# One step of a hybrid GLA and HGRN2 decoder layer: the first norm's gain applied by feature out of PSUM, the low-rank unit in two passes, one diagonal step, levels in 32 columns

## What is computed

```python
h  = x + rms_norm(token_mix(rms_norm(x, norm_mix_pre)), norm_mix_post)
x' = h + rms_norm(swiglu(rms_norm(h, norm_ffn_pre)), norm_ffn_post)
```

```python
S_t = diag(a_t) S_{t-1} + k_t^T v_t ;  o_t = q_t S_t
scores[t, s] = sum_k q[t,k] k[s,k] exp(b[t,k] - b[s,k])   for s <= t, b = cumsum(log a)
```

## Time and profile before

| what | us |
|---|---|
| median of 3 runs | 1134.85 |
| lowest, highest | 1133.91, 1137.36 |
| the profiled execution | 1134.5 |
| its span | 1132.7 |
| PE (matmul) busy in it | 1084.6 |
| DVE busy | 680.1 |
| ACT busy | 479.9 |
| POOL busy | 51.2 |

### The profile page before, as it was taken

How to read it: one execution, slowest core, us unless ns; L and a number is a source line. 1 busy time by engine, 2 the same in 40 slices (tenths; PEclk the granted TensorE clock), 3 DMA queues, 4 the chain that set the end, 5 groups by cost and what they waited for, 6 DMA issues and landing times.

```text
span 1132.7 us, 24821 instructions
## 1 busy us (share of the span) xinstructions
PE 1084.6 (96%) x10860; PEld 1020.0 (90%) x10860; DVE 680.1 (60%) x977; ACT 479.9 (42%) x765; POOL 51.2 (5%) x78
## 2 busy tenths in 40 slices
PE   4999999999999999999999999789999999999998
PEld 4999999989999899999899977689999999988886
DVE  4255543565444655525655457699999999854544
ACT  4342244523335522445333443653444444533432
POOL 6000000100001000001000011000000000000000
PEclk8999999999999999999999999899999999999999
DMA  6532232522224522235222155024243333332212
GB/s 174 135 83 55 72 84 81 164 74 59 75 67 123 142 56 76 67 94 167 58 76 76 48 170 175 1 76 112 77 112 84 104 94 94 99 106 75 93 56 84
DMA packets 138619, 105.19 MB, mean 93 GB/s; under 512 B 3968, under 2 KB 123776, under 8 KB 138512
## 3 DMA queue, kind: packets, MB, share of 16 engines
q1 hardware_dynamic: 133648, 85.78, 26.9%
...
...
## 4 chain that ended last, share of the span: by engine, by line
PE 88%; DVE 6%; ACT 2%; DVEq 1%; ACTq 1%; issue 1%; DMA 1%; POOL 0%; POOLq 0%
PE ps L253 42%; PE ps L1663 19%; PE ps L1685 12%; PE ps L342 2%; PE ps L935 2%; PE ps L989 1%; PE ps L966 1%; PE ps L956 1%; PE ps L911 1%; PE ps L968 1%; PE ps L973 1%; PE ps L931 1%; ACT w_hi_t L239 1%; DVE w_lo_t L243 1%; PE ps L949 1%
## 5 line engine op out<-in xcount | busy, mean ns | idle before, releaser
L253 PE MATMUL ps<-x_hi,w_lo_t 128*128 128x288 f32 x1168 | 258.3, 303 | 4.1 <-DVE w_lo_t L243 4.1
L253 PE MATMUL ps<-x_lo,w_hi_t 128*128 128x288 f32 x1168 | 252.6, 298 | 0.0
L253 PE MATMUL ps<-x_hi,w_hi_t 128*128 128x288 f32 x1168 | 252.5, 298 | 0.0
L239 ACT ACTIVATE w_hi_t<-w_raw_t 128x1024 fp32r<-128x1024 f32 x73 | 77.2, 1058 | 353.3 <-PE ps L253 341.8
L243 DVE TENSOR_TENSOR w_lo_t<-w_raw_t,w_hi_t 128x1024 fp32r<-128x1024 f32 x75 | 91.7, 1222 | 188.2 <-ACT w_hi_t L239 188.2
L253 PEld LDWEIGHTS ps<-x_hi,w_lo_t 128*128 128x128 f32 x1168 | 189.5, 192 | 9.1 <-DVE w_lo_t L243 4.2
L253 PEld LDWEIGHTS ps<-x_hi,w_hi_t 128*128 128x128 f32 x1168 | 190.7, 191 | 0.0
L253 PEld LDWEIGHTS ps<-x_lo,w_hi_t 128*128 128x128 f32 x1168 | 190.5, 191 | 0.0
L1663 PE MATMUL ps<-x_hi,w_lo_t 128*128 128x288 f32 x264 | 78.7, 298 | 5.5 <-issue 4.1
L1663 PE MATMUL ps<-x_lo,w_hi_t 128*128 128x288 f32 x264 | 78.4, 297 | 0.0
L1663 PE MATMUL ps<-x_hi,w_hi_t 128*128 128x288 f32 x264 | 78.4, 297 | 0.0
...
## 6 DMA issues: line engine op xcount, KB each, us to landing
w_raw_t<-in_w_in_dram SPq DMA_DIRECT2D x73, 512.0 KB, 3.8
merged<-in_w_ffn_in_dram SPq DMA_DIRECT2D x22, 512.0 KB, 5.1
w_raw_t<-in_w_ffn_in_dram SPq DMA_DIRECT2D x22, 512.0 KB, 4.7
w_raw_t<-in_w_ffn_out_dram SPq DMA_DIRECT2D x22, 512.0 KB, 3.7
h_t<-in_x_prompt_dram SPq DMA_DIRECT2D x8, 512.0 KB, 6.0
...
h_t<-in_state_hgrn_dram POOLq DMA_DIRECT2D x8, 512.0 KB, 8.4
...
```

What stands on the lines that cost most here:

```text
L239: nc.scalar.activation(w_hi_t[:, u % NSPL, 0:nk, :], w_raw_t[:, u % NRAW, 0:nk, :], ACT.Copy).then_inc(w_hi, 1)
L253: m = nc.tensor.matmul(out[:, q, :], w[:, u % NSPL, k, :], x(k, q), start=first and i == 0, stop=last and i == len(todo) - 1)
```

## The change

1. *Gain.* The diagonals and their spreading over the partitions are gone. POOL multiplies a tile by 1/rms in place. PE transposes it, and DVE multiplies the transposed tile by the gain, which is then one number per partition and block k, from PSUM into SBUF (`gained_x`, in buffers that are unused so far). `x_hi` and `x_lo` are made from that. ACT's `x_hi` of tile c now comes after the squares of tile c + 3 (`LAG`), not c + 2.
2. *Low-rank unit.* POOL writes the low part of the 16 weights beside the high part in the same 128 columns (columns 16 to 31). So two passes, x_lo and x_hi, give high and low products in 32 rows; the decay matmul sums them with `wlr4` standing twice. It runs token tile by token tile (80 matmuls) into banks 6 and 7.
3. *Order of the start.* Unit 0's weights are loaded before the last token tile, unit 1's right behind it. POOL splits both units (high and low), between and after its scalings, and makes the masks last.
4. *Diagonal.* One step in place of three, its 54 matmuls packed in one PSUM slot by strips; DVE takes it in six copies.
5. *Levels 5 and 6.* Level 6 in matmuls of 32 columns, twice as many; in both, every second head lands in the other half of the partitions, so that all four strips are used. DVE takes them in twice as many copies of half the size.

```diff
-NOW = {2: ["decay"], 6: ["diag0", "diag1", "diag2"], 7: ["level0", "v0"], 8: ["level1", "v1"], 9: ["level2", "v2"],
+NOW = {2: ["decay"], 6: ["diag"], 7: ["level0", "v0"], 8: ["level1", "v1"], 9: ["level2", "v2"],
...
-    glr = A("glr", [GR, T])
-    wlr4 = A("wlr4", [GR, GH * P])
+    glr = A("glr", [2 * GR, T])
+    wlr4 = A("wlr4", [2 * GR, GH * P])
...
-    gains = O[:, :, :].rearrange("p a b -> p (a b)")[:, 0:D].rearrange("p (k n) -> p k n", k=KT)
-    gain_rows = ps[:, 6:8, :].rearrange("p a b -> p (a b)")
+    glr_out = ps[:, 6:8, :].rearrange("p a b -> p (a b)")
+    x_full = [t[:, :, :].rearrange("p a b -> p (a b)")[:, i * D:(i + 1) * D] for t, i in ((O, 0), (O, 1), (Gt, 0), (Gt, 1), (Q, 0))]
+
+    def gained_x(c):
+        return x_full[c][:, 0:KT * tok(c)].rearrange("p (k t) -> p k t", k=KT)
...
         for c in range(NT):
+            if c == NC:
+                load_unit(sp, 0, win_v[:, :, GLR:GLR + P])
             sp.dma_start(xt[c][0:tok(c), :], xp_v[c] if c < NC else xs_v).then_inc(x_in[c], 16)
-        load_unit(sp, 0, win_v[:, :, GLR:GLR + P])
+        load_unit(sp, 1, win_v[:, :, UNITS[0][0]:UNITS[0][0] + P])
...
+                     (onm[:, 0:2], gla_onorm), (onm[:, 2:3], hgrn_onorm), (blr4[:, :], gla_b_lr),
+                     (wlr4[0:GR, :], gla_w_lr2.rearrange("o r d -> (o r) d")), (wlr4[GR:2 * GR, :], gla_w_lr2.rearrange("o r d -> (o r) d"))):
...
+                if j == 0 and n == 0:
+                    continue
...
 
+        for c in range(NT):
+            if c == NC:
+                pool.wait_ge(w_raw[0], loaded(0))
+                nc.gpsimd.tensor_copy(w_hi_t[:, 0, :, :], w_raw_t[:, 0, :, :]).then_inc(w_hi, 1)
+                pool.wait_ge(w_hi, 1)
+                nc.gpsimd.tensor_tensor(w_hi_t[:, 0, :, GR:2 * GR], w_raw_t[:, 0, :, 0:GR], w_hi_t[:, 0, :, 0:GR].bitcast(F32),
+                                        ALU.subtract).then_inc(w_lo, 2)
+            pool.wait_ge(squared, c + 1)
+            nc.gpsimd.tensor_scalar(xt[c][0:tok(c), :], xt[c][0:tok(c), :], stat[0:tok(c), 1, c:c + 1], None, ALU.mult).then_inc(scaled, 1)
+        pool.wait_ge(w_raw[1], loaded(1))
+        nc.gpsimd.tensor_copy(w_hi_t[:, 1, :, :], w_raw_t[:, 1, :, :]).then_inc(w_hi, 1)
+        pool.wait_ge(w_hi, 2)
+        nc.gpsimd.tensor_tensor(w_lo_t[:, 1, :, :], w_raw_t[:, 1, :, :], w_hi_t[:, 1, :, :].bitcast(F32), ALU.subtract).then_inc(w_lo, 1)
         pool.wait_ge(consts, n)
-        pool.wait_ge(gain_in, 16)
-        for k in range(KT):
-            nc.gpsimd.tensor_scalar(gains[:, k, :], ident[:], gain[:, 0, k:k + 1], None, ALU.mult).then_inc(gain_diag, 1)
...
-        for u in range(2):
-            pool.wait_ge(w_raw[u % NRAW], loaded(u))
-            nc.gpsimd.tensor_copy(w_hi_t[:, u % NSPL, :, :], w_raw_t[:, u % NRAW, :, :]).then_inc(w_hi, 1)
...
-        for i in range(NT + 2):
+        for i in range(NT + LAG):
...
-            if i >= 2:
-                c = i - 2
-                act.wait_ge(turned, c + 1)
-                act.activation(x_hi[:, :, tokens(c)], turned_x(c), ACT.Copy).then_inc(x_hi_s, 1)
-        act.wait_ge(small, 16 * 5)
+            if i >= LAG:
+                c = i - LAG
+                act.wait_ge(gained, c + 1)
+                act.activation(x_hi[:, :, tokens(c)], gained_x(c), ACT.Copy).then_inc(x_hi_s, 1)
+        act.wait_ge(small, 16 * 6)
...
-        act.activation(halves(glr[:, :]), proj(0)[0:GR], ACT.Copy).then_inc(unit_free, 1)
+        act.activation(glr[:, :], glr_out[0:2 * GR, 0:T], ACT.Copy).then_inc(unit_free, 1)
...
+                    if j == 0:
+                        act.wait_ge(consts, CONSTS)
...
-        dve.drain().then_inc(w_lo, 1)
...
-        dve.wait_ge(gain_row, 1)
-        for i in range(NT + 2):
+        dve.wait_ge(gain_in, 16)
+
+        def gain_x(c):
+            dve.wait_ge(turned, c + 1)
+            dve.tensor_tensor(gained_x(c), turned_x(c), gain[:, 0, :].rearrange("p (k o) -> p k o", o=1).broadcast_to([P, KT, tok(c)]),
+                              ALU.mult).then_inc(gained, 1)
+
+        for i in range(NT + LAG - 1):
             if i < NT:
-                n = tok(i)
-                dve.wait_ge(squared, i + 1)
-                dve.scalar_tensor_tensor(xt[i][0:n, :], xt[i][0:n, :], stat[0:n, 1, i:i + 1], gain_rows[0:n, :],
-                                         ALU.mult, ALU.mult).then_inc(scaled, 1)
-            if i >= 2:
-                c = i - 2
+                gain_x(i)
+            if i >= LAG - 1:
+                c = i - LAG + 1
                 dve.wait_ge(x_hi_s, c + 1)
-                dve.tensor_tensor(x_lo[:, :, tokens(c)], turned_x(c), x_hi[:, :, tokens(c)].bitcast(F32), ALU.subtract).then_inc(x_lo_s, 1)
-            if i >= NT - 1 and i <= NT:
-                dve.wait_ge(w_hi, i - NT + 2)
-                split_lo(i - NT + 1)
-        dve.wait_ge(small, 16 * 5)
+                dve.tensor_tensor(x_lo[:, :, tokens(c)], gained_x(c), x_hi[:, :, tokens(c)].bitcast(F32), ALU.subtract).then_inc(x_lo_s, 1)
+        dve.wait_ge(small, 16 * 6)
         dve.wait_ge(w_hi, 3)
         split_lo(2)
...
-        dve.wait_ge(consts, CONSTS)
...
             if L >= 32:
                 for t in range(0, C, 2 * L):
-                    ins = dve.tensor_copy(Am[t:t + L, :, t + L:t + 2 * L],
-                                          s[t:t + L, 0:3 * NC * C // 2].rearrange("p (h r) -> p h r", r=C // 2)[:, :, t // 2:t // 2 + L])
+                    for up in (0, 1):
+                        ins = dve.tensor_copy(Am[t:t + L, up:3 * NC:2, t + L:t + 2 * L],
+                                              s[t + up * L:t + up * L + L, 0:3 * NC // 2 * L].rearrange("p (h r) -> p h r", r=L))
...
-        def diagonal(j, i):
-
-            s = step(j, f"diag{i}")
+        def diagonal(j):
+
+            s = step(j, "diag")
             one = ident[:, :].bitcast(I32).rearrange("p (o t) -> p o t", o=1)
-            if i < 2:
-                ins = dve.copy_predicated(Am[:, 6 * i:6 * i + 6, :], one.broadcast_to([P, 6, C]),
-                                          s[:, 0:6 * C].rearrange("p (h t) -> p h t", t=C))
-            else:
-                ins = dve.copy_predicated(As[:, :, :], one[0:TS, :, 0:TS].broadcast_to([TS, 3, TS]),
-                                          s[0:TS, 0:3 * TS].rearrange("p (h t) -> p h t", t=TS))
-            freed(ins, j, f"diag{i}")
+            for t in range(0, C, STRIP):
+                strip = slice(t, t + STRIP)
+                got = s[strip, 0:3 * NT * STRIP].rearrange("p (h t) -> p h t", t=STRIP)
+                if t < TS:
+                    dve.copy_predicated(As[strip, :, strip], one[strip, :, strip].broadcast_to([STRIP, 3, STRIP]), got[:, 3 * NC:3 * NT, :])
+                ins = dve.copy_predicated(Am[strip, :, strip], one[strip, :, strip].broadcast_to([STRIP, 3 * NC, STRIP]), got[:, 0:3 * NC, :])
+            freed(ins, j, "diag")
...
-                    for i in range(3):
-                        diagonal(j, i)
+                    if j == 0:
+                        dve.wait_ge(consts, CONSTS)
+                    diagonal(j)
                     dve.tensor_tensor(Q[:, :, :], Q[:, :, :], Z[:, :, :], ALU.mult).then_inc(lvl, 1)
...
-        pe.wait_ge(gain_diag, KT)
-        for k in range(KT):
-            m = nc.tensor.matmul(gain_rows[:, k * P:(k + 1) * P], ones[:, :], gains[:, k, :], start=True, stop=True)
-        m.then_inc(gain_row, 1)
-        for c in range(NT):
+        pe.wait_ge(consts, 5)
+
+        def turn_x(c):
             n = tok(c)
             pe.wait_ge(scaled, c + 1)
             if c >= 3:
-                pe.wait_ge(x_lo_s, c - 2)
+                pe.wait_ge(gained, c - 2)
             for k in range(KT):
                 m = nc.tensor.transpose(turned_x(c)[:, k, :], xt[c][0:n, k * P:(k + 1) * P], ident[0:n, 0:n])
             m.then_inc(turned, 1)
+
+        def low_rank(c):
+            pe.wait_ge(x_lo_s, c + 1)
+            for k in range(KT):
+                for x in (x_lo, x_hi):
+                    m = nc.tensor.matmul(glr_out[:, tokens(c)], w_hi_t[:, 0, k, :], x[:, k, tokens(c)],
+                                         start=k == 0 and x is x_lo, stop=k == KT - 1 and x is x_hi, skip_group_check=True)
+            return m
+
+        for c in range(NC):
+            turn_x(c)
         pe.wait_ge(w_lo, 2)
-        pe.wait_ge(x_lo_s, NT)
-        pe.wait_ge(consts, CONSTS)
-        unit_passes(0, proj(0), xh, xl).then_inc(unit_done, 1)
+        low_rank(0)
+        turn_x(NC)
+        for c in range(1, NT):
+            m = low_rank(c)
+        m.then_inc(unit_done, 1)
...
-            elif name[:4] == "diag":
-                i = int(name[4:])
-                if i == 0:
-                    pe.wait_ge(qk_in, j + 1)
-                for a in range(6 if i < 2 else 3):
-                    c, h = divmod(6 * i + a, 3)
-                    width = C if i < 2 else TS
-                    for t in range(0, width, STRIP):
+            elif name == "diag":
```

(13 more changed lines are left out.)

4 lines of the change are left out of this document (1 added, 3 removed).

## The result

Four executions of the changed kernel have a median of **1121.55 us** (1120.99 to 1123.28), those of the kernel before, on the same chip, 1136.11 us (1133.91 to 1137.42). The ratio is 0.9876, with a 95% interval of 0.9854 to 0.9898. So the change is faster, by 1.2%, but 11.5 us short of the forecast of 1110 us, and outside its range of 1105 to 1119 us. The profiled execution took 1120.99 us, with a span of 1119.3 us: 13.4 us less than the 1132.7 us before.

A forecast was written before the change was run, and what follows sets the result against it. TensorE, busy 96% of the span, was taken as the bound, so only less work or less idling helps. 1134.5 - 9.3 (start) - 10.6 (diagonal) - 4.8 (levels) = 1109.8, plus 0.35 for the median: 1110 us, range 1105 to 1119 us.

The forecast's parts named there:

- Start. ... Unit 1 starts at 25.2 us: -9.3 us: Start of the kernel: unit 1 would begin at 25.2 us instead of 34.53 us, a gain of 9.3 us.
- I take 1.6 us: Start, POOL's row scale: 1.6 us for each tile, chosen near the cast, between 1.04 and 4.75 us.
- Rival A: Start: POOL slow at the row scale, 3.5 us a tile; start gains only 1.5 us, total 1117.9 us; chance 0.15.
- Between 0.056 us and 0.107 us I take 0.09 us: Start, low-rank unit: one narrow matmul takes 0.09 us, so 1.4 us a tile.
- I charge 1 us: Start: a piece at TensorE's lower clock, 1.2 GHz, is expected again and costs 1 us; before it cost 2.7 us.
- DVE at 1.22 us for each x_lo: Start, DVE's queue: each operation, including a tile's x_lo, takes 1.22 us, or 0.68 us for tile 4.
- Diagonal: -10.6 us: Diagonal step: one piece without waiting for DVE saves 2.66 us in each of four groups, 10.6 us.
- rival C: Level 0 waits for DVE because strip copies are dearer; 7.2 us come back, total 1117 us; chance 0.06.
- Levels: -4.8 us: Levels 5 and 6: matmuls over four column groups save 1.2 us in each of four groups, 4.8 us.
- rival B: Levels 5 and 6: small matmuls cost issue, not columns, so the levels give nothing; 1114.9 us; chance 0.1.
- the worse end of the start: Start: POOL at 3.5 us a tile and low-rank matmuls at 0.107 us, gaining only about 0.4 us.

The follow-up runs named there:

- warm_pe: The changed kernel with TensorE kept busy at the start by unread matmuls, six before the first turn and one behind each of the first four: 1120.76 us.
- lr32: The changed kernel with the low-rank matmuls loading only the 32 stationary columns that hold weights, not 128: 1113.77 us.
- masks_late_warm: dve_scale_lr32 with POOL's masks behind the last x_lo, four unread matmuls before the first turn and two behind tile 4's turn: 1108.09 us.
- dve_scale_lr32: The changed kernel with the row scale on DVE and only 32 stationary columns loaded in the low-rank unit: 1107.99 us.
- dve_scale: The changed kernel with the row scale done by DVE, one tile ahead of its gain multiplication, and not by POOL: 1118.17 us.
- w1_dve: masks_late_warm with the low part of unit 1's weights taken by DVE, not POOL: 1105.85 us.
- diag_only: The kernel before with only the diagonal made one step: 1119.71 us.
- diag_wait: The changed kernel with TensorE made to wait behind the diagonal step for DVE's last copy of it: 1144.35 us.

## Why the prediction was wrong

The direction and two of its three terms held. The step that failed is **"Start. ... Unit 1 starts at 25.2 us: -9.3 us"**: it starts at 39.66 us, and unit 1 to the decay step took 20.6 us where it took 18.9 us before. Four things in that sum were mis-sized.

1. *"I take 1.6 us" for POOL's row scale.* It takes 2.84 us. My bounds (1.04 to 4.75 us) held it, but I chose the value by likeness to the cast, when the one row of the same operation, L403's 594 ns for 128 columns, was there. With it 2.84 us means 2.5 ns an element and 0.27 us fixed. Four in a row cost 5 us more than I had. Rival A named this (3.5 us a tile), with a chance of 0.15 and nothing for the low-rank side.
2. *"Between 0.056 us and 0.107 us I take 0.09 us" for a low-rank matmul.* It takes 0.213 us, outside both bounds. My upper bound was right for the full clock (0.11 us in warm_pe), and lr32 shows that the weight load sets it, not the moving side. But both bounds were full-clock numbers. The Trainium skill, "TensorE: Matmul & The Clock Gate", section "LDWEIGHTS (loading the stationary operand)", which makes a load go by its columns alone, 107 ns for 128 of them, was the better guide: warm_pe's 0.11 us agrees. It gives no second figure for the low clock, where these rows doubled. Loads and subtraction taken together (1.24 us for 128 elements, where I had 0.5 us from L450), the low-rank unit ran from 21.15 to 39.66 us instead of 15.5 to 24.2 us.
3. *"I charge 1 us" for the clock.* In the change TensorE stays at 1.2 GHz until 42.5 us: already the eight loads of a turn take 1.57 us, where they took 0.86 us. The extra 0.1 us on each of 80 low-rank matmuls is 8 us, and unit 1 to the decay step takes 1.3 us more (20.60 us against 19.27 us at full clock in masks_late_warm). I looked at when the clock fell in the kernel before and not at what had brought it up. There the 16 dense gain matmuls of L885 stood from 7.3 to 11.1 us, three turns followed 1.2 us apart, and the clock was full for them. But that the missing gain matmuls keep it low is not shown: dve_scale_lr32 has none either, nor fillers, and with turns 1.8 us apart its third and fourth are at full clock,

```profile
14.06 0.86 PEld L912 LDWEIGHTS ps<-ident,h_t 128*128 128x128 f32 x8 [0.93 <-DVE h_t L671]
```

while in the change POOL's scaling sets them 2.8 us apart. And a clock brought up early didn't stay up: it fell at 17.9 us before and at 25.2 us in warm_pe.
4. *DVE at 1.22 us for each x_lo.* Before, x_lo read PSUM and SBUF; now both operands lie in SBUF, and beside POOL it took 1.35 and 1.70 us, and 3.10 us for two. The change itself doesn't pay for it, since PE is later; lr32 and what follows do.

Each has a run or row of its own: (1) by the row and by dve_scale, (2) by lr32, (3) in its size by warm_pe's two paces and the 288-column pace in the change, its cause being open, (4) by w1_dve. What warm_pe leaves open is what the start would cost if the clock held through the 128-column loads: it wasn't to be had.

**Diagonal: -10.6 us** held exactly as a count of waits (none left), and 0.12 us for 12 more records is 0.14 us by the row. Level 0 doesn't wait for DVE: rival C is out. What the term left out is the clock behind three of the waits, 4.5 us in the profiled execution. diag_only (-16.3) and diag_wait (+22.8) both show it. I had even used the low clock's price at the start, and never looked at windows behind the four waits. It was luck for the total: the start alone is 16.1 us off its forecast (+6.85 for -9.3 us), the kernel only 11.5 us.

**Levels: -4.8 us** is -4.2 us. Level 5 came to 0.52 us (0.47 expected), level 6 to 0.71 us (0.65). Narrow matmuls on four column groups do run side by side; rival B is out. The Trainium skill's 60 cycles a matmul ("TensorEngine Tiling (Array Packing)", section "Instruction Overhead"), taken as a price for one record after the other as in the prediction, don't fit: 108 records in 1.08 us are 10 ns each, or 20 ns for each of the 54 matmuls, where 60 cycles at 2.4 GHz would be 25 ns, by estimate. Inside one column group, though, a record takes 40 ns, so these rows say nothing against 60 cycles there.

My range reached to rival A and to the worse end of the start (-0.4 us), and that end did take both risks together: POOL at 3.5 us and matmuls at 0.107 us "at the low clock". POOL was faster than that. What broke the range is that 0.107 us is the full clock's figure; at the low clock a low-rank matmul took 0.213 us, and one chain runs through POOL and all of them.
